# Decoder trunk step: the squares of k as two fp32r halves for their product with ones, and work reordered around it

## The chip, the cores and the metric

The kernel runs on one core of a Trainium2 chip. The metric is the device time of one execution in microseconds (us), median of the runs shown. TensorE multiplies matrices, VectorE (DVE), ScalarE (ACT) and GpSimd (POOL) do the elementwise work, SyncE (SP) issues the transfers. Each engine works through its own instructions in order, and semaphores order the engines against each other.

## The reference

One layer of a hybrid decoder for 512 prompt tokens and 8 x 8 sample tokens (576 columns), width 1024, 8 heads. What the change touches:

```python
qkv = jax.nn.silu(causal_dwconv(qkv_ext, conv_qkv_w))
k = l2norm(qkv[..., QK_WIDTH:2 * QK_WIDTH].reshape(B, L, N_HEADS, HEAD_K))
def l2norm(x):
    return x * lax.rsqrt(jnp.sum(x * x, axis=-1, keepdims=True) + EPS)
o, s_new = gated_delta_chunked(q, k, v, g, beta, s_delta)   # chunked delta rule per head
glu = glu_in[..., :CONF_WIDTH] * jax.nn.sigmoid(glu_in[..., CONF_WIDTH:])
c = causal_dwconv(conf_ext, conf_dw_w) + conf_dw_b          # 31 taps
```

Around it stand the input projection (1024 to 3072 + 16 + 5120 columns), a gated output norm per head, a LayerNorm with swish on the convolution branch, the output projection and a feed-forward block of 4096 with squared relu.

## The kernel before

Activations lie with channels on the 128 partitions and the 576 tokens along the row. Every dense product is made in a split form: both operands are cut into a high fp32r half and a low fp32r rest, and three products (high x high, low weights x high, high weights x low) are summed in PSUM. A job is one block of 128 output channels: 8 blocks of the inner dimension, 3 products, two halves of 288 columns, 48 products of TensorE. The weights' high half is a cast on ScalarE (`proj_split`, L1060), the low half a subtraction on GpSimd (L2026, 2.4 us).

**Passes.** After a first stage that projects head 1's inputs (`raw_job`), passes 1 to 8 follow. Pass n does the attention of head n while it projects the inputs of head n + 1, convolves them, and evacuates the gates of head n. Pass 1 and pass 8 are written out, passes 2 to 7 are one loop, on every engine. Each pass is a list of slots s = 0 to 31. In each slot TensorE first issues as many dense products as `MIDDLE_AT[s]` says (12, 12, 14, 14, ...), and then the small products of that slot (`phase`, from L705). The other engines walk through the same slots in the same order, each with its own conditions on s; the order is written out by hand.

**Around the product with ones** (the boundary of two passes):

- slot 29, TensorE: last state products (L846, L848). ScalarE copies the output o and squares it in PSUM (L1300, L1302).
- slot 30: DVE adds the q term to the squares (`o_sq`) and updates the sample states; then taps of the 31-tap convolution (`conf_taps`, L1605, counts per slot in `late` and `late_1`).
- slot 31: TensorE sums o's squares with a matrix of ones (`ones_sum`, L632, full fp32). ScalarE squares k (`square_k`, L1148), then takes the logarithm and the exponent that give o's factor; DVE scales o (`head_out`), then more taps.
- slot 0 of the next pass: TensorE sums k's squares with ones (L632, two full fp32 products of 288 columns). ScalarE, once `head_out` and the sums are there, makes k's factor (L1243, L1245). DVE copies the head's columns (L1799) and writes kn = kc * factor (L1655).
- slot 2: TensorE transposes kn (L722) and v (L700); in pass 1 v's transposes stand in slot 7. ScalarE copies v (L1248).

**Around slots 20 to 23.** In slot 20 GpSimd splits weights, then writes `gext`, the gated convolution input (L2167, L2168), and signals `gext_ready`. In slot 22 TensorE multiplies gk with u (L813) and the first chunk (L832); ScalarE negates and copies that into kn (L1270, `kd_ready`) and scales the chunk (`chunk_u`, L1184, `u_ready`). In slot 23 TensorE's first state product (L846) waits for both; the sample products (L858) follow.

**Entry of pass 1.** The last things of the first stage are DVE's read of v's projection and its 4-tap convolution (`read_qkv`, `qkv_conv`), and GpSimd's low halves of the input (`in_low`). TensorE's first job of pass 1 waits per block k for `in_ready`, and after 12 of its products for that read of v.

Of the kernel before, what the change touches and what calls it, by code (L numbers as in the profile page):

```python
# [25 lines left out]
F32 = mybir.dt.float32  # L26
# [5 lines left out]
P = 128  # L32
HP = P // 2
D = 1024
H = 8
# [45 lines left out]
_LAYOUT = [("zero", 1), ("ident", P), ("ident2", HP), ("ones", P), ("tri", P), ("suf", P), ("tri_s", SMP), ("suf_s", SMP),  # L81
# [14 lines left out]
def build(nc, x_t, w_all, w_log, log_par, consts, params, taps, halos, s_in,  # L96
          y_out, s_prompt, s_sample, qkv_rows, conf_rows):
    with ExitStack() as ctx:
# [3 lines left out]
        def sem(name):  # L102
# [9 lines left out]
                 ("gext", GXT + NS * GXS), ("c4", TOK), ("c31", TOK),  # L112
# [51 lines left out]
        csum = sb("csum", TOK)  # L164
        q_sq = sb("q_sq", TOK)
# [155 lines left out]
        k_sq, k_sums, k_scale, k_ready = sem("k_sq"), sem("k_sums"), sem("k_scale"), sem("k_ready")  # L321
# [245 lines left out]
        def _(pe):  # L567
# [22 lines left out]
            def dense(n, s):  # L590

                done = sum(spread(n)[:s])
                for i in range(done, done + spread(n)[s]):
                    j, r = divmod(i, PASS_MM)
                    h, r = divmod(r, PASS_MM // 2)
                    k, p3 = divmod(r, 3)
                    at, w = base(n) + j, w_buf(n, j)
                    if r == 0:
                        if h == 0:
                            pe.wait_ge(w_high, at + 1)  # L600
                            pe.wait_ge(w_low, at + 1)
                        if last(n) and j == 8:
                            pe.wait_ge(ln_scaled, KB)
                        elif last(n) and j == 9:
                            pe.wait_ge(act_read, 2 * at - 3 + h)
                        elif n_is(n, 1) and j == 0:
                            pe.wait_ge(pair_read, 4)
                        else:
# [17 lines left out]
            def ones_half(dst, src, start=True, stop=True):  # L626
                return mm(dst, con("ones"), src, start=start, stop=stop)

            def ones_sum(dst, src, start=True, stop=True):

                for h in range(2):
                    r = mm(dst[:, h], con("ones"), src[:, h * HALF:(h + 1) * HALF],  # L632
                           start=start, stop=stop)
                return r
# [70 lines left out]
            def phase(n):  # L705
                for s in range(32):
# [335 lines left out]
        def _(act):  # L1042
# [102 lines left out]
            def square_k(n):  # L1145

                act.wait_ge(act_conv, 3 * n + turn(n, 1) + 1)
                A(v["vt"][:, 0:TOK], v["kc"], ACT.Square).then_inc(k_sq, 1)  # L1148

# [42 lines left out]
            def phase(n):  # L1192
                for s in range(33):
# [52 lines left out]
                    if s == (7 if n_is(n, 1) else 2):  # L1246
                        act.wait_ge(kv_tr, 2 * n)
                        A(v["vt"][:, 0:SEQ], g(1), ACT.Copy)  # L1248
                        A(v["vts"][0:SMP], g(3)[0:SMP, 0:P], ACT.Copy).then_inc(vt_ready, 1)
# [4 lines left out]
                    if s in range(8, 19, 2):  # L1254
# [9 lines left out]
                        r.then_inc(x_ready, 1)  # L1264
                        if s == 8 and not last(n):
# [60 lines left out]
            square_k(0)  # L1326
# [145 lines left out]
        def _(dve):  # L1472
# [10 lines left out]
            ve.memset(v["gext"][:, 0:CF_TAPS - 1], 0.0)  # L1483
            ve.memset(csum[:], 0.0).then_inc(csum_done, 1)
# [130 lines left out]
            def qkv_conv(n, i, a, b):  # L1615
# [19 lines left out]
                if b == QK_TAPS:  # L1635
                    if i == 0 and not first(n):
                        dve.wait_ge(qd_ready, n)
                    dve.wait_ge(conv4_prod, 3 * n + at + 1)
                    ve.tensor_reduce(CONV[i][:, SEQ:TOK].rearrange("p (s a) -> p s a", s=NS), products(at),  # L1639
                                     mybir.AxisListType.X, ALU.add).then_inc(conv4, 1)  # L1640
                    dve.wait_ge(conv4, 15 * n + 5 * at + 5)
                    dve.sem_inc(conv4_done, 1)
# [114 lines left out]
            late_1 = {24: 4, 25: 2, 26: 3, 27: 2, 28: 2, 29: 1, 30: 4, 31: 4}  # L1757
            early_1 = {1: 3, 2: 1, 3: 3, 8: 2, 10: 1, 12: 1, 16: 1, 18: 1, 19: 2, 20: 2, 21: 2}

            def convolutions(n, s):  # L1760
                proj = not last(n)
                rest = early_8 if last(n) else early_1 if n_is(n, 1) else early
# [259 lines left out]
        def _(pool):  # L2022
# [83 lines left out]
            for k in range(4, KB):  # L2106
                in_low(k)
            pool.wait_ge(in_ready, KB)
# [5 lines left out]
            pool.wait_ge(act_read, 10)  # L2114
            qkv_rows_and_products(0, 2)
# [21 lines left out]
            def phase(n):  # L2137
# [6 lines left out]
                for s in range(33):  # L2144
# [73 lines left out]
                    if s == 19:  # L2218
# [3 lines left out]
                        tt(pr(v["um"]), pr(t_r.bitcast(F32)), bc(con("ident")), ALU.subtract).then_inc(tmi_ready, 1)  # L2222
                    if s == 26:
# [63 lines left out]
def shape_constants():  # L2287
# [15 lines left out]
    put("ones", np.ones((P, P)))  # L2303
# [100 lines left out]
```

## Time and profile before

| | us |
|---|---|
| median of 3 runs | 1101.4 |
| lowest and highest | 1097.24 and 1102.29 |
| the profiled execution | 1099.08 |
| its span in the trace | 1097.1 |

| engine | busy us | share of the span |
|---|---|---|
| PE (TensorE) | 1076.4 | 98% |
| DVE | 709.8 | 65% |
| ACT | 508.2 | 46% |
| POOL | 578.1 | 53% |

The profile is of one execution; its time is 2.3 us under the median. The mean granted clock of TensorE was 0.995 of full. A row of a timeline has the start in us, the length in us, the engine and line, the output and inputs by name, the shapes, a count, and in brackets the idle time ahead of it with what ended it. PE is TensorE's products, PEld its weight loads. A product of 288 columns is recorded about 0.3 us long, and the next one starts before it ends: the distance of starts is what it costs. A full fp32 product leaves two records.

### The profile page before, as it was taken

What the parts mean: (1) busy time and instruction counts of PE and PEld (TensorE: products, weight loads), DVE (VectorE), ACT (ScalarE), POOL (GpSimd) and SP (SyncE); (2) the same over time, 40 slices, a digit from 0 to 9 for tenths busy, and PEclk for the clock granted to TensorE, in tenths of its full rate; (3) what the DMA queues carried; (4) which work ended last, traced back from release to release, by engine and by line L of the source; (5) the groups of instructions that cost most, each with busy time, mean ns of one, the idle gap of its engine ahead of it and who ended that gap; (6) DMA issues with size and microseconds to landing.
All of it is one profiled execution on the core that took longest, in us unless ns stands there. A gap on an engine that the chain in (4) does not pass through costs nothing.

```text
span 1097.1 us, 22165 instructions
## 1 busy us (share of the span) xinstructions
PE 1076.4 (98%) x8279; PEld 1054.0 (96%) x8279; DVE 709.8 (65%) x1150; ACT 508.2 (46%) x918; POOL 578.1 (53%) x503
## 2 busy tenths in 40 slices
PE   8999999999999999999999999999999999999996
PEld 6899899999999999999999999999999999999996
DVE  7987987969879698797967757631243134216635
ACT  7844455554554555545746955321232123214531
POOL 1987385583855738557574432324333433436831
PEclk9999999999999999999999999999999999999998
DMA  6223112231122311223221252122232222223302
GB/s 239 95 65 108 62 40 90 80 106 61 38 90 78 106 61 42 86 78 106 81 73 44 64 218 77 59 78 77 78 94 80 78 83 89 76 76 96 98 21 86
DMA packets 32663, 92.12 MB, mean 84 GB/s; under 512 B 4704, under 2 KB 12256, under 8 KB 32608
## 3 DMA queue, kind: packets, MB, share of 16 engines
q1 hardware_dynamic: 32608, 91.36, 25.8%
q8 instruction: 38, 0.62, 0.2%
q14 instruction: 17, 0.14, 0.0%
HBM read 82.83 MB, written 8.52 MB: 83 GB/s over the span
## 4 chain that ended last, share of the span: by engine, by line
PE 87%; DVE 5%; issue 2%; ACT 1%; POOL 0%; DVEq 0%; ACTq 0%
PE ps L584 31%; PE ps L613 30%; PE ps L622 6%; PE ps L977 5%; DVE ps L1479 2%; DVE work L1476 1%; PE ps L805 1%; PE ps L858 1%; PE ps L795 1%; PE ps L774 1%; PE ps L867 1%; PE ps L832 1%; PE ps L813 1%; PE ps L846 1%; PE ps L848 1%
## 5 line engine op out<-in xcount | busy, mean ns | idle before, releaser
L2026 POOL TENSOR_TENSOR w_lo<-raw,w_hi 128x1024 fp32r<-128x1024 f32 x121 | 292.4, 2417 | 360.6 <-ACT w_hi L1078 231.0
L613 PE MATMUL ps<-in_hi,w_hi 128*128 128x288 f32 x944 | 287.6, 305 | 0.6 <-POOL in_lo L2026 0.6
L613 PE MATMUL ps<-in_hi,w_lo 128*128 128x288 f32 x944 | 284.4, 301 | 0.0
L613 PE MATMUL ps<-in_lo,w_hi 128*128 128x288 f32 x944 | 283.0, 300 | 0.0
L1479 DVE SCALAR_TENSOR_TENSOR ps<-work,ct,ps 128x512 f32<-128x512 f32 x240 | 180.7, 753 | 7.3 <-DVE work L1639 1.5
L613 PEld LDWEIGHTS ps<-in_hi,w_hi 128*128 128x128 f32 x944 | 178.0, 189 | 1.9 <-POOL in_lo L2026 0.9
L613 PEld LDWEIGHTS ps<-in_hi,w_lo 128*128 128x128 f32 x944 | 177.8, 188 | 0.9
L613 PEld LDWEIGHTS ps<-in_lo,w_hi 128*128 128x128 f32 x944 | 178.0, 189 | 0.2
L1078 ACT CAST w_hi<-raw 128x1024 fp32r<-128x1024 f32 x61 | 63.8, 1048 | 224.2 <-PE ps L584 224.2
L1476 DVE TENSOR_TENSOR f_tmp<-f_tmp 128x576 f32<-128x576 f32 x31 | 70.7, 2281 | 96.3 <-ACT f_tmp L1426 91.0
L1476 DVE TENSOR_TENSOR o_a<-o_a,ps 128x576 f32<-128x576 f32 (+1 forms) x40 | 25.3, 634 | 144.8 <-PE ps L584 122.8
L584 PE MATMUL ps<-in_hi,w_hi 128*128 128x288 f32 x464 | 99.4, 296 | 0.1
L584 PE MATMUL ps<-in_lo,w_hi 128*128 128x288 f32 x464 | 99.4, 296 | 0.0
L584 PE MATMUL ps<-in_hi,w_lo 128*128 128x288 f32 x464 | 99.3, 296 | 0.0
L584 PE MATMUL ps<-f_lo,w_hi 128*128 128x288 f32 x384 | 82.5, 296 | 0.0
L584 PE MATMUL ps<-f_hi,w_hi 128*128 128x288 f32 x384 | 82.5, 296 | 0.0
L584 PE MATMUL ps<-f_hi,w_lo 128*128 128x288 f32 x384 | 82.5, 296 | 0.0
L584 PEld LDWEIGHTS ps<-in_hi,w_hi 128*128 128x128 f32 x464 | 74.7, 189 | 0.3 <-issue 0.3
L584 PEld LDWEIGHTS ps<-in_hi,w_lo 128*128 128x128 f32 x464 | 74.8, 189 | 0.0
L584 PEld LDWEIGHTS ps<-in_lo,w_hi 128*128 128x128 f32 x464 | 74.7, 189 | 0.0
L1060 ACT CAST w_hi<-raw 128x1024 fp32r<-128x1024 f32 x63 | 65.6, 1042 | 0.0
L584 PEld LDWEIGHTS ps<-f_hi,w_hi 128*128 128x128 f32 x384 | 61.8, 189 | 0.0
(312 smaller groups left out, 2291.9 us busy)
## 6 DMA issues: line engine op xcount, KB each, us to landing
raw<-w_all_in SPq DMA_DIRECT2D x135, 512.0 KB, 3.6
work<-s_in_in SPq DMA_DIRECT2D x8, 512.0 KB, 3.2
s_sample_out<-work SPq DMA_DIRECT2D x8, 512.0 KB, 2.7
xt<-x_t_in SPq DMA_DIRECT2D x4, 576.0 KB, 6.7
xt<-x_t_in SPq DMA_DIRECT2D x2, 1152.0 KB, 7.1
y_out<-o_a SPq DMA_DIRECT2D x16, 144.0 KB, 1.7
halo<-halos_in SPq DMA_DIRECT2D x9, 156.0 KB, 3.5
conf_rows_out<-c_rows SPq DMA_DIRECT2D x8, 135.0 KB, 2.1
```

The source lines that it names most:

```text
L584: r = mm(ps[:, 2 * w + h, 0:HALF], a[:, k], b[:, k, h * HALF:(h + 1) * HALF], start=k == 0 and p3 == 0, stop=k == KB - 1 and p3 == 2)
L613: t = mm(dense_ps(n, j, h), a[:, w, k], b[:, k, h * HALF:(h + 1) * HALF], start=r == 0, stop=r == PASS_MM // 2 - 1)
L622: r = mm(dst, a[:, k], half_of(b[:, k], h), start=k == 0 and p3 == 0, stop=k == KB - 1 and p3 == 2)
L774: r = mm(tile(g(0), c)[0:HP], cut(w, c), tile(t_r, c), start=True, stop=True)
L795: r = mm(tile(g(0), c)[0:HP], cut(uc_r, c), tile(x_r, c), start=True, stop=True)
L805: r = mm(cut(g(1), c), tile(x_r, c), cut(uc_r, c), start=True, stop=True)
L977: r = mm(half_ps(i % 4), a[:, k], half_of(b[:, k], h), start=k == 0 and p3 == 0, stop=k == KB - 1 and p3 == 2)
L1060: nc.scalar.copy(w_hi[:, w_buf(n, j)], raw[:, raw_slot(n, j)]).then_inc(w_high, 1)
L1078: nc.scalar.copy(weight(m, off)[0], raw[:, (off + 2) % RING]).then_inc(w_high, 1)
L1476: return ve.tensor_tensor(out, a, b, op)
L1479: return ve.scalar_tensor_tensor(out=out, in0=a, scalar=s_, in1=b, op0=op0, op1=op1)
L2026: return gp.tensor_tensor(out, a, b, op)
```

## The change

From pass 2 on the squares of k are formed in slot 21 (24 in pass 1) of the pass before: ScalarE writes them twice, as fp32r (`ksq_hi`, on the place of c4) and as fp32 (on the place of extk), GpSimd subtracts in slot 22 (25) to get the low half (`ksq_lo`, on the place of c31), and TensorE sums four fp32r products. The square in slot 31 is gone. The places require waits: the squares for `gext_ready`, the subtraction for `conf_ready`, the halo copies for the product with ones.

With it come: the matrix of ones is set by DVE instead of loaded; in the first half of pass 1's first job the 16 products with the high input come first and wait for `high_ready`, the 8 with the low input last; v's transposes in pass 1 stand in slot 8, and its copies behind those of the first level; v's sample sum (`qkv_samples`) and one tap stand behind kn in slot 0 of pass 1, and one tap more behind v's convolution; pass 1 has 18 of its own taps in place of 22, and pass 2, now written out on DVE, takes the other four in slots 8, 10, 12 and 16; GpSimd forms v's sample products ahead of its memsets.

```diff
@@ dense (TensorE)
+                    low_last = n_is(n, 1) and j == 0 and h == 0
+                    if low_last:
+                        k, p3 = divmod(r, 2) if r < 2 * KB else (r - 2 * KB, 2)
...
-                    if n_is(n, 1) and j == 0 and h == 0 and p3 == 0:
+                    if low_last and p3 == 0:
+                        pe.wait_ge(high_ready, k + 1)
+                    if low_last and p3 == 2:
                         pe.wait_ge(in_ready, k + 1)
@@ TensorE
+            def ones_pair(dst, hi, lo):
+                for h in range(2):
+                    mm(dst[:, h], ones_r[:], half_of(hi, h), start=True, stop=False)
+                    r = mm(dst[:, h], ones_r[:], half_of(lo, h), start=False, stop=True)
                 return r
...
-                        ones_sum(g2(0), v["vt"]).then_inc(k_sums, 1)
+                        if n_is(n, 1):
+                            ones_sum(g2(0), v["vt"]).then_inc(k_sums, 1)
+                        else:
+                            ones_pair(g2(0), ksq_hi, ksq_lo).then_inc(k_sums, 1)
...
-                    if n_is(n, 1) and s == 7:
+                    if n_is(n, 1) and s == 8:
                         pe.wait_ge(act_conv, 3)
                         pe.wait_ge(qk_ready, 1)
                         v_transposes()
@@ ScalarE
+            def square_k_pair(n):
+                act.wait_ge(act_conv, 3 * n + 3)
+                act.wait_ge(gext_ready, n + 1)
+                A(ksq_hi[:], v["kc"], ACT.Square)
+                A(ksq, v["kc"], ACT.Square).then_inc(k_high, 1)
...
+            def v_tile(n):
+                act.wait_ge(kv_tr, 2 * n)
+                A(v["vt"][:, 0:SEQ], g(1), ACT.Copy)
+                A(v["vts"][0:SMP], g(3)[0:SMP, 0:P], ACT.Copy).then_inc(vt_ready, 1)
...
+                        if s == 8 and n_is(n, 1):
+                            v_tile(n)
                         if s == 8 and not last(n):
                             conv_silu(n, 0)
+                    if s == (24 if n_is(n, 1) else 21) and not last(n):
+                        square_k_pair(n)
                     if s == 22:
...
                     if s == 31 and not last(n):
                         log_exp()
-                        square_k(n)
@@ DVE
+            ve.memset(ones_r[:].bitcast(F32), 1.0)
...
-            late_1 = {24: 4, 25: 2, 26: 3, 27: 2, 28: 2, 29: 1, 30: 4, 31: 4}
-            early_1 = {1: 3, 2: 1, 3: 3, 8: 2, 10: 1, 12: 1, 16: 1, 18: 1, 19: 2, 20: 2, 21: 2}
+            late_1 = {24: 4, 25: 2, 26: 3, 27: 2, 28: 2, 29: 1, 30: 2, 31: 2}
+            early_1 = {1: 3, 2: 1, 3: 3, 8: 2, 10: 1, 12: 1, 16: 1, 18: 1, 19: 2, 20: 2, 21: 1}
+            early_2 = {1: 3, 2: 1, 3: 3, 8: 3, 10: 1, 12: 1, 16: 1}
...
+                    if n_is(n, 1) and s == 0:
+                        dve.wait_ge(in_ready, KB)
                     head(n, s)
+                    if n_is(n, 1) and s == 0:
+                        conf_taps(0, 12, 13)
+                        qkv_samples(0, 2)
...
-            conf_taps(0, 10, 12)
+            conf_taps(0, 10, 11)
             read_qkv(2)
             qkv_conv(0, 2, 0, QK_TAPS)
+            conf_taps(0, 11, 12)
             phase(1)
-            with dve.Fori(2, H) as n:
+            phase(2)
+            with dve.Fori(3, H) as n:
@@ GpSimd
+            pool.wait_ge(act_read, 10)
+            qkv_rows_and_products(0, 2)
             pool.wait_ge(in_ready, KB)
...
                         pool.wait_ge(conv4_done, 3 * n)
+                        pool.wait_ge(k_sums, n)
                         pool.nop(nofuse=True)
                         halo_copies(n)
...
+                    if s == (25 if n_is(n, 1) else 22) and proj:
+                        pool.wait_ge(k_high, n)
+                        pool.wait_ge(conf_ready, n)
+                        tt(ksq_lo[:], ksq, ksq_hi[:].bitcast(F32), ALU.subtract).then_inc(k_sq, 1)
```

## Rows read from the trace of the kernel before

**Rows 1.** the chain of work that ended last: L858 in three passes (start us, us, what)
```profile
106.54 1.69 PE ps L858 x16
...
178.45 1.69 PE ps L858 x16
...
246.47 1.69 PE ps L858 x16
```

**Rows 2.** timeline of TensorE in slot 0 of pass 3 (start us, us, engine, line)
```profile
195.52 1.14 PE L632 MATMUL ps<-work,cst 128*128 128x288 f32 x4
...
196.63 0.29 PE L613 MATMUL ps<-in_hi,w_lo 128*128 128x288 f32 x1
...
196.76 0.29 PE L613 MATMUL ps<-in_lo,w_hi 128*128 128x288 f32 x1
```

**Rows 3.** timeline, end of pass 2 to slot 2 of pass 3, and the wait one pass later
```profile
191.98 0.82 DVE L1476 TENSOR_TENSOR work<-ps,q_sq 128x512 f32<-128x512 f32 x2 [0.44 <-ACT ps L1302]
...
200.23 0.66 PE L722 MATMUL ps<-cst,work 128*128 128x128 f32 x4
...
201.92 0.30 PE L613 MATMUL ps<-in_hi,w_hi 128*128 128x288 f32 x1
...
268.23 0.42 PEld L722 LDWEIGHTS ps<-cst,work 128*128 128x128 f32 x4 [0.35 <-DVE work L1476]
```

**Rows 4.** timeline of DVE and TensorE between pass 1 and pass 2
```profile
122.28 3.12 DVE L1479 SCALAR_TENSOR_TENSOR ps<-work,ct,ps 128x512 f32<-128x512 f32 x4
...
126.83 3.12 DVE L1479 SCALAR_TENSOR_TENSOR ps<-work,ct,ps 128x512 f32<-128x512 f32 x4
...
127.98 0.29 PE L613 MATMUL ps<-in_hi,w_lo 128*128 128x288 f32 x1
...
130.76 1.12 PE L722 MATMUL ps<-cst,work 128*128 128x128 f32 x4 [2.49 <-DVE work L1476]
...
133.89 0.29 PE L613 MATMUL ps<-in_hi,w_hi 128*128 128x288 f32 x1
```

**Rows 5.** engines' busy time by stretch; last three: granted clock, DMA share, GB/s
```profile
49.00:58.40 9.40, 6.91 (x45) 5.92 (x43) 6.60 (x13) 6.46 (x9) 9.34 (x13) 1.00 0.29 94
...
130.70:133.90 3.20, 3.13 (x15) 3.06 (x16) 3.10 (x6) 0.70 (x2) 2.39 (x7) 0.51 0.05 18
```

**Rows 6.** timeline of TensorE and GpSimd at the entry of pass 1
```profile
51.60 1.21 PE L632 MATMUL ps<-work,cst 128*128 128x288 f32 x4 [0.62 <-DVE work L1476]
...
54.62 0.40 PE L613 MATMUL ps<-in_hi,w_hi 128*128 128x288 f32 x1 [0.63 <-POOL in_lo L2026]
...
56.90 2.36 POOL L2026 TENSOR_TENSOR w_lo<-raw,w_hi 128x1024 fp32r<-128x1024 f32 x1
...
58.37 0.66 PE L722 MATMUL ps<-cst,work 128*128 128x128 f32 x4 [1.22 <-DVE work L1476]
...
60.30 0.29 PE L613 MATMUL ps<-in_hi,w_hi 128*128 128x288 f32 x1
...
72.06 0.63 PE L700 MATMUL ps<-cst,work 128*128 128x128 f32 x4 [0.87 <-DVE work L1476]
```

**Rows 7.** timeline of slots 20 to 23 of pass 2, all engines
```profile
174.83 1.55 POOL L2026 TENSOR_TENSOR work<-work 128x512 f32<-128x512 f32 x2
...
176.16 0.60 ACT L1270 ACTIVATE work<-ps 128x512 f32<-128x512 f32 x1 [4.72 <-PE ps L814]
...
176.41 0.75 DVE L1602 TENSOR_SCALAR ps<-work,ct 128x512 f32<-128x512 f32 x1 [1.84 <-POOL work L2026]
...
176.76 0.37 ACT L1184 ACTIVATE work<-ps,hc 128x128 f32<-128x128 f32 x1
...
177.71 0.32 PEld L846 LDWEIGHTS ps<-work 128*128 128x128 f32 x2
```

**Rows 8.** timeline of ScalarE, slot 31 of pass 2
```profile
193.58 0.69 ACT L1148 ACTIVATE work<-work 128x576 f32<-128x576 f32 x1
...
194.17 0.72 ACT L1307 ACTIVATE work<-ps,cst 128x576 f32<-128x576 f32 x1
```

More of the change, by code:

```diff
@@ L78 @@
 STORE_ORDER = (range(8), (3, 4, 0, 5, 1, 6, 7, 2))
-_LAYOUT = [("zero", 1), ("ident", P), ("ident2", HP), ("ones", P), ("tri", P), ("suf", P), ("tri_s", SMP), ("suf_s", SMP),
+_LAYOUT = [("zero", 1), ("ident", P), ("ident2", HP), ("tri", P), ("suf", P), ("tri_s", SMP), ("suf_s", SMP),
            ("eps", 1), ("epsq", 1), ("big", P), ("big_s", SMP), ("lvl", (LEVELS - 1) * HP),
@@ L111, in build @@
                  ("extq", EXT + NS * EXS), ("extk", EXT + NS * EXS), ("extv", EXT + NS * EXS),
-                 ("gext", GXT + NS * GXS), ("c4", TOK), ("c31", TOK),
+                 ("gext", GXT + NS * GXS + 1), ("c4", TOK), ("c31", TOK),
                  ("qc", TOK), ("kc", TOK), ("vc", TOK),
@@ L164, in build @@
         csum = sb("csum", TOK)
+        ones_r = sb("ones_r", P, F32R)
+        ksq_hi = nc.alloc_sbuf_tensor_at("ksq_hi", [P, TOK], F32R, offset=work_at + 4 * (5 * SEQ + starts["c4"]))
+        ksq_lo = nc.alloc_sbuf_tensor_at("ksq_lo", [P, TOK], F32R, offset=work_at + 4 * (5 * SEQ + starts["c31"]))
+        ksq = v["extk"][:, 4:4 + TOK]
         q_sq = sb("q_sq", TOK)
@@ L320, in build @@
         hc_ready, gm_ready, w_part_landed = sem("hc_ready"), sem("gm_ready"), sem("w_part_landed")
-        k_sq, k_sums, k_scale, k_ready = sem("k_sq"), sem("k_sums"), sem("k_scale"), sem("k_ready")
+        k_high, k_sq, k_sums, k_scale, k_ready = sem("k_high"), sem("k_sq"), sem("k_sums"), sem("k_scale"), sem("k_ready")
         conv4_prod = sem("conv4_prod")
@@ L595, in dense @@
                     h, r = divmod(r, PASS_MM // 2)
-                    k, p3 = divmod(r, 3)
+                    low_last = n_is(n, 1) and j == 0 and h == 0
+                    if low_last:
+                        k, p3 = divmod(r, 2) if r < 2 * KB else (r - 2 * KB, 2)
+                    else:
+                        k, p3 = divmod(r, 3)
                     at, w = base(n) + j, w_buf(n, j)
@@ L626, in ones_half @@
             def ones_half(dst, src, start=True, stop=True):
-                return mm(dst, con("ones"), src, start=start, stop=stop)
+                return mm(dst, ones_r[:].bitcast(F32), src, start=start, stop=stop)
             def ones_sum(dst, src, start=True, stop=True):
                 for h in range(2):
-                    r = mm(dst[:, h], con("ones"), src[:, h * HALF:(h + 1) * HALF],
+                    r = mm(dst[:, h], ones_r[:].bitcast(F32), src[:, h * HALF:(h + 1) * HALF],
                            start=start, stop=stop)
+                return r
+            def ones_pair(dst, hi, lo):
+                for h in range(2):
+                    mm(dst[:, h], ones_r[:], half_of(hi, h), start=True, stop=False)
+                    r = mm(dst[:, h], ones_r[:], half_of(lo, h), start=False, stop=True)
                 return r
@@ L716, in phase @@
                         pe.wait_ge(k_sq, n)
-                        ones_sum(g2(0), v["vt"]).then_inc(k_sums, 1)
+                        if n_is(n, 1):
+                            ones_sum(g2(0), v["vt"]).then_inc(k_sums, 1)
+                        else:
+                            ones_pair(g2(0), ksq_hi, ksq_lo).then_inc(k_sums, 1)
                     if s == 2:
@@ L1143, in conv_silu, with square_k @@
                 A(CONV[i][:, SEQ:TOK], CONV[i][:, SEQ:TOK], ACT.Silu).then_inc(act_conv, 1)
-            def square_k(n):
-                act.wait_ge(act_conv, 3 * n + turn(n, 1) + 1)
+            def square_k():
+                act.wait_ge(act_conv, 1)
                 A(v["vt"][:, 0:TOK], v["kc"], ACT.Square).then_inc(k_sq, 1)
+            def square_k_pair(n):
[3 more added lines that the diff above has]
+                A(ksq, v["kc"], ACT.Square).then_inc(k_high, 1)
             def square_q(n):
@@ L1245, in phase @@
                         A(g2(0), two(v["at"]), ACT.Exp, scale=-0.5).then_inc(k_scale, 1)
[L1246 to L1249, printed above, removed]
+                    if s == 2 and not n_is(n, 1):
+                        v_tile(n)
                     if s == 3:
@@ L1264, in phase @@
                         r.then_inc(x_ready, 1)
+                        if s == 8 and n_is(n, 1):
+                            v_tile(n)
                         if s == 8 and not last(n):
                             conv_silu(n, 0)
+                    if s == (24 if n_is(n, 1) else 21) and not last(n):
+                        square_k_pair(n)
                     if s == 22:
@@ L1325, in _ @@
             conv_silu(0, 1)
-            square_k(0)
+            square_k()
             read_by_dve(4)
@@ L1634, in qkv_conv, with qkv_samples @@
                     stt(out, e[:, t:t + SEQ], w, out, ALU.mult, ALU.add).then_inc(conv4, 1)
[L1635 to L1642, printed above, removed]
+                if b == QK_TAPS and not (first(n) and i == 2):
+                    qkv_samples(n, i)
+            def qkv_samples(n, i):
+                at = turn(n, i)
+                if i == 0 and not first(n):
+                    dve.wait_ge(qd_ready, n)
+                dve.wait_ge(conv4_prod, 3 * n + at + 1)
+                ve.tensor_reduce(CONV[i][:, SEQ:TOK].rearrange("p (s a) -> p s a", s=NS), products(at),
+                                 mybir.AxisListType.X, ALU.add).then_inc(conv4, 1)
+                dve.wait_ge(conv4, 15 * n + 5 * at + 5)
+                dve.sem_inc(conv4_done, 1)
             def sample_state(n):
@@ L1756, in _ @@
             late = {22: 2, 23: 2, 24: 4, 25: 2, 26: 2, 27: 2, 28: 2, 29: 1, 30: 3, 31: 2}
-            late_1 = {24: 4, 25: 2, 26: 3, 27: 2, 28: 2, 29: 1, 30: 4, 31: 4}
-            early_1 = {1: 3, 2: 1, 3: 3, 8: 2, 10: 1, 12: 1, 16: 1, 18: 1, 19: 2, 20: 2, 21: 2}
+            late_1 = {24: 4, 25: 2, 26: 3, 27: 2, 28: 2, 29: 1, 30: 2, 31: 2}
+            early_1 = {1: 3, 2: 1, 3: 3, 8: 2, 10: 1, 12: 1, 16: 1, 18: 1, 19: 2, 20: 2, 21: 1}
+            early_2 = {1: 3, 2: 1, 3: 3, 8: 3, 10: 1, 12: 1, 16: 1}
             def convolutions(n, s):
                 proj = not last(n)
-                rest = early_8 if last(n) else early_1 if n_is(n, 1) else early
+                rest = early_8 if last(n) else early_1 if n_is(n, 1) else early_2 if n_is(n, 2) else early
                 if s in rest:
@@ L2113, in _ @@
             gate_rows()
-            pool.wait_ge(act_read, 10)
-            qkv_rows_and_products(0, 2)
             proj_split(1, 1)
@@ L2302, in shape_constants @@
     put("ident2", i[:, :HP] % HP == j[:, :HP])
-    put("ones", np.ones((P, P)))
     put("tri", i <= j)
```

## The prediction

> **What bounds the kernel now.** I read the chain that ended last first: the sixteen small products of the sample state (L858) stand in it once per pass, 71.91 us apart from pass 1 to 2 and 68.02 us from 2 to 3 [rows 1]. Later passes repeat the 68.0 us, so the first step is 3.9 us longer. TensorE is busy nearly all of the span, so the question is what TensorE waits for, and second, whether work taken off it lies where it would wait anyway.
>
> The steady boundary of two passes, as TensorE sees it: product of k's squares with ones in slot 0, 26 dense products, then the transposes of the scaled k (L722), which wait 0.35 us on the DVE product that writes kn [rows 3]. That product is the end of a row of DVE work without a hole: from 191.98 (the first add of the output's squares, which waits for ScalarE's square of o, itself released by the last state product of slot 29) to about 200.2, where TensorE starts [rows 3]. Nothing in it waits for the product with ones.
>
> The same place between pass 1 and 2 is worse: four taps at 122.28 and four at 126.83 stand in DVE's row, TensorE stops for 2.49 us, and its next rows take 3.13 us (130.76 to 133.89) where pass 3 takes 1.69 us (200.23 to 201.92) [rows 3, 4]. The window over that stretch shows the granted clock at 0.51, the lower level of 1.2 GHz [rows 5]. At the entry of pass 1 there are three waits (0.62, 0.63, 1.22 us) and one of 0.87 us at the transposes of v [rows 6], all at a granted clock of 1.00 [rows 5].
>
> **The change, part by part.**
>
> *The product itself.* In the old form, from 195.52 to 196.63 lie the four records of two full fp32 products and one dense product; dense products follow each other at 0.13 us (196.63 to 196.76; over longer stretches 0.133). So the two cost 1.11 - 0.13 = 0.98 us [rows 2]. Four fp32r products of the same shape are four dense steps, 0.53 us. That frees 0.45 us of TensorE in each of seven passes. In passes 3 to 8 this is worth nothing: TensorE comes to the transposes of k 0.45 us earlier and waits 0.35 + 0.45 = 0.80 us for the same kn [rows 3]. If that cover were absent it would be 6 x 0.45 = 2.7 us. I take 0, and keep 2.7 for the range. (The Trainium skill, FP8 and Floating Point Precision, section TensorE Precision Notes, says a true fp32 product is four passes through the array. By that the two would be eight passes of 288 columns against four: an estimate of 0.48 us saved at 2.4 GHz, against 0.45 from the rows. The page alone, without asking who waits next, would give 7 x 0.48 = 3.4 us off the time. That is a rival below.)
>
> *The squares move on ScalarE.* In slot 31 one square goes; ScalarE's result is not waited for there (DVE's row has no hole there), so 0. In slot 21 (24 in pass 1) two squares come in, behind a wait for the gated values gext. This I take to be the costly step. In the steady pass gext ends at 174.83 + 1.55 = 176.38, and DVE, which waits for the same semaphore, starts at 176.41 [rows 7]. ScalarE's next work now starts at 176.16: kn's negated copy, and 0.60 us behind it the first chunk of u, done at 177.13 [rows 7]. TensorE wants both at 177.71, for the first state product [rows 7]. With the pair in front, the squares start at 176.42, each 0.59 us behind the other (193.58 to 194.17 for such a square [rows 8]), so the copy starts at 177.60, u is there at 178.57, and TensorE goes on at about 178.63: a wait of 0.92 us. Behind it on ScalarE come a table load and the reads of z, which have over a microsecond of room. All later steps of the pass hang on TensorE, DVE's taps too, and the end chain is counted from slot 29, so nothing gives the 0.92 back. Six passes (2 to 7): +5.5 us. Bounds: 0 if the pair finds gext earlier, and +6.4 if a square with fp32r output has a pitch of 0.67. In pass 1 the pair stands in slot 24, in a hole of 1.39 us ahead of the second chunk: 0.
>
> *The low half on GpSimd*: one subtraction of 1.4 us in slot 22 (25 in pass 1), where GpSimd is idle for some 4.8 us ahead of its next weight split; it hides there. Its result is wanted 15 us later. The halo copies' wait for the product with ones is over by the time they are due.
>
> *DVE's taps.* Pass 1 loses four taps of 0.78 us in slots 30 and 31, and pass 2 takes them in slots 8, 10, 12 and 16, where DVE waits 0.4 to 1.1 us for TensorE; pass 1 already carries such taps there without stopping it. The tap moved from slot 21 has room too. At the boundary: o is scaled at 123.84 instead of 125.31, head_out at 125.4, two taps to 126.95, kn from 127.05 to 127.75. TensorE gets there at 127.98 + 0.13 - 0.45 = 127.7. So the transposes start near 127.8 instead of 130.76: 2.97 us. With no long stop the clock stays up: 3.13 - 1.69 = 1.44 us more [rows 3, 4]. Together -4.4 us; bounds -2.5 and -4.4.
>
> *Entry of pass 1.* One tap less ahead of v's read: the wait of 0.62 goes. High products first in the first half: at 54.62 only one product of three is left, 0.27 us. kn no longer stands behind v's sample sum, which waited for GpSimd: it runs from 54.65 to 55.4, and TensorE arrives at 56.74 instead of 58.37, 1.63 us ahead. But the low weights of the second job still end at 56.90 + 2.36 = 59.26 on GpSimd, and that job's first product (60.30 before) would now be due at 58.67: a new wait of 0.7, and 0.94 us are left [rows 6]. The wait of 0.87 at v's transposes goes (slot 8). The copies of v now stand behind the first level's copies on ScalarE and hold TensorE in slot 9 for about 0.5. Sum -1.2 us; bounds -0.3 (the low weights and v's copies later than I think) and -2.5.
>
> *Ones from a memset, a longer DVE program, a smaller constants transfer*: at the start, where other loads end last: 0.
>
> Sum: -1.2 - 4.4 + 5.5 = -0.1 us on the profiled 1099.1 us (span 1097.1), which lies 2.3 us below the median of 1101.4. I forecast 1101.3. The bounds together: -0.3 - 2.5 + 6.4 = +3.6, so 1105; and -2.5 - 4.4 - 2.7 + 0 = -9.6, so 1091.8.
>
> **Rivals.** About 0.5% (5.5 us) is what a measurement can tell here; the three runs of before are 5 us apart.
>
> A. *The pair costs nothing on ScalarE.* For: ScalarE has 4.7 us idle ahead of the copy. Against: that hole ends before gext does [rows 7]. Then only the gains: 1101.4 - 5.6 = 1095.8, right at the bound. Chance 0.17.
>
> B. *The product's gain counts in each pass as well* (the page's sum, 3.4 us, or mine of 0.45 x 7 less the one already counted). It needs a shorter DVE row at the boundary. Against: that row is not touched in the loop. With A, 1101.4 - 5.6 - 2.7 = 1093; without A, 1098.6, no change by the bound. Chance 0.05 with A, 0.04 alone.
>
> C. *The clock falls once a pass.* TensorE would wait 0.9 us in slot 23, and near 0.25 and 0.8 at the boundary. If those drop the clock as the 2.49 us stop did, each pass pays 1.44 us more: 6 x 1.44 = 8.6, so 1110, slower. It decides from four such passes on. Against: 1.22 us alone, with two of 0.6 before it inside 7 us, left the clock at 1.00 [rows 5, 6]. Chance 0.07. (The Trainium skill, TensorE: Matmul & The Clock Gate, section A second HAM failure mode, says that frequent small idles between groups of products can make the clock go back and forth. No row here shows that; rows show only the fall after 2.49 us.)
>
> D. *The rebalancing fails*: the four taps in pass 2 stop TensorE there, or the stop at the boundary stays, and ScalarE's wait comes on top. +5.5 - 1.2 and perhaps +1: 1106, about the bound. Chance 0.09.
>
> The forecast has 0.58. Faster: half of A and B with A, and a little, 0.15. Slower: C and a third of D, 0.11. The same: 0.74. The range runs from A to D, 1095.5 to 1106.0, some 0.83.
>
> **What the changed profile would show.** The small products of slot 23 about 68.9 us apart in passes 2 to 7 (68.0 if A), with a wait of TensorE of 0.9 us at the first state product in slot 23, released by ScalarE, and an idle time on ScalarE ahead of the squares that ends on GpSimd; the wait at the transposes of k near 0.8 us; pass 2 no longer at clock 0.51; a wait on GpSimd's weights near 59 us and on ScalarE's copy of v near 75 us. Wrong would be: no wait in slot 23, or a clock under 1.00 in the loop.

## The result and the profile after

The changed kernel takes 1105.7 us (median of 20 runs, 1101.3 to 1110.3), the kernel before, in runs between them on the same chip, 1101.5 us (20 runs, 1097.2 to 1102.4). The ratio is 1.0040 with a 95% interval of 1.0027 to 1.0053: slower by 4 us, beyond the interval, though under the 0.5% that the text called measurable. The forecast was 1101.3, the same. The profiled execution took 1101.7 us (span 1099.9) at a granted clock of 0.993; that of before had 1099.1, 1097.1 and 0.995. So the two profiled executions lie 2.6 us apart, the medians 4.2. The account by trace below is of these two executions; both are among the short ones of their kernel, and no profile here is of an execution near either median.

The chain that ended last, of the changed kernel (start us, us, what). The small products of slot 23 are L878 here, L858 in [rows 1]; they are eight fp32 products of 16 columns, which leave sixteen records:

```profile
105.42 1.69 PE ps L878 x16
...
174.28 1.69 PE ps L878 x16
...
243.18 1.69 PE ps L878 x16
...
313.68 1.69 PE ps L878 x16
...
382.58 1.69 PE ps L878 x16
...
451.50 1.69 PE ps L878 x16
...
522.01 1.69 PE ps L878 x16
...
602.47 1.69 PE ps L878 x16
```

The first line is 1.12 us earlier than in [rows 1]. The step from pass 1 to 2 is 68.86 and no longer 71.91: the slow boundary is gone. The next steps are 68.90 where 68.0 stood, and two of them, from 243.18 and from 451.50, are 70.50.

What the weight loads of TensorE waited for, all passes (us in total, times, longest), the lines of slot 23 and of k's transposes:

```profile
PEld ps L866 <- ACT work L1211: 5.2, 6, 0.9
PEld ps L742 <- DVE work L1509: 4.1, 5, 0.8
```

Six waits of 0.87 us on ScalarE, at the first state product. The timeline of pass 3 around slot 23, against [rows 7] one pass earlier:

```profile
238.66 1.55 POOL L2073 TENSOR_TENSOR work<-work 128x512 f32<-128x512 f32 x2
...
240.24 0.76 DVE L1636 TENSOR_SCALAR ps<-work,ct 128x512 f32<-128x512 f32 x1 [1.83 <-POOL work L2073]
240.30 0.69 ACT L1174 ACTIVATE ksq_hi<-work 128x576 fp32r<-128x576 f32 x1 [5.03 <-POOL work L2073]
...
240.89 0.67 ACT L1175 ACTIVATE work<-work 128x576 f32<-128x576 f32 x1
...
241.47 0.58 ACT L1304 ACTIVATE work<-ps 128x512 f32<-128x512 f32 x1
...
242.05 0.37 ACT L1211 ACTIVATE work<-ps,hc 128x128 f32<-128x128 f32 x1
...
242.47 0.49 PE L866 MATMUL ps<-work 128*128 128x128 f32 x2 [0.63 <-ACT work L1211]
...
243.02 1.86 PE L878 MATMUL ps<-work 128*128 128x16 f32 x16
...
245.34 0.30 PE L623 MATMUL ps<-in_hi,w_lo 128*128 128x288 f32 x1
...
245.47 0.40 PE L623 MATMUL ps<-in_lo,w_hi 128*128 128x288 f32 x1
...
245.68 0.44 PE L623 MATMUL ps<-in_hi,w_hi 128*128 128x288 f32 x1
...
245.91 0.44 PE L623 MATMUL ps<-in_hi,w_lo 128*128 128x288 f32 x1
```

This is the queue that was forecast: both squares start when GpSimd's gated values are there, 0.59 us behind each other, the negated copy (L1304) and the chunk of u (L1211) behind them, and TensorE behind that. The last four lines are what was not forecast: dense products step by 0.13 us up to 245.47 (from 245.34), and then by 0.21 and 0.23.

The windows of that stretch and of pass 6, and of the old slow boundary (columns as in [rows 5]):

```profile
246.00:248.00 2.00, 2.00 (x11) 2.00 (x11) 1.93 (x3) 0.46 (x2) 0.00 (x0) 0.50 0.00 0
...
454.00:456.00 2.00, 2.00 (x11) 2.00 (x10) 1.93 (x3) 0.33 (x1) 0.00 (x0) 0.50 0.00 0
128.00:131.00 3.00, 3.00 (x26) 3.00 (x25) 2.97 (x7) 0.69 (x2) 0.89 (x5) 1.00 0.24 91
```

The clock falls to its lower level of 1.2 GHz (0.50 of full) for a while from 245.5 and again some 210 us later, in two passes of six, and each fall costs 70.50 - 68.90 = 1.60 us. The boundary of [rows 5], at 0.51 before, runs at 1.00.

The account by trace, to the last L878: -1.1 (first line), -3.9 (the 71.91 that became a normal 68.0), +5.3 (six waits), +3.2 (two falls), -0.1 in the last step: +3.4, measured 602.47 - 599.06 = 3.4. Behind it the changed kernel is 0.6 shorter, so the span is 2.8 longer.

### The profile page after: what moved, and what is told of

Read it like the earlier page. It is cut to its first block, busy times and chain, and to the rows that moved or that the text cites. A ratio compares the mean times of both kernels' runs of the same rounds, so it can differ in the third digit from the quotient of the medians.

```text
span 1099.9 us, 22125 instructions
## 1 busy us (share of the span) xinstructions
PE 1076.0 (98%) x8279; PEld 1053.8 (96%) x8279; DVE 709.3 (64%) x1151; ACT 512.2 (47%) x925; POOL 588.9 (54%) x510
## 4 chain that ended last, share of the span: by engine, by line
PE 79%; POOL 6%; issue 5%; DVE 4%; ACT 3%; DVEq 0%; ACTq 0%; POOLq 0%
PE ps L588 31%; PE ps L623 25%; PE ps L632 6%; PE ps L997 5%; POOL w_lo L2073 2%; DVE ps L1512 2%; POOL work L2073 2%; PE ps L878 1%; POOL o_a L2073 1%; PE ps L825 1%; DVE work L1509 1%; POOL in_lo L2073 1%; PE ps L866 1%; PE ps L887 1%; PE ps L815 1%
## 5 line engine op out<-in xcount | busy, mean ns | idle before, releaser
L588 PEld LDWEIGHTS ps<-f_hi,w_lo 128*128 128x128 f32 x384 | 61.8, 189 | 0.0
```

The source lines that it names most:

```text
L588: r = mm(ps[:, 2 * w + h, 0:HALF], a[:, k], b[:, k, h * HALF:(h + 1) * HALF], start=k == 0 and p3 == 0, stop=k == KB - 1 and p3 == 2)
```

## The experiments

"Behind" and "ahead" are places in ScalarE's order. Runs of the kernel before between them gave medians of 1101.9, 1101.8 and 1101.3.

**1. The squares behind the chunk of u.** From pass two on the pair is issued in slot 22 behind the first chunk.

```diff
-                    if s == (24 if n_is(n, 1) else 21) and not last(n):
+                    if n_is(n, 1) and s == 24:
                         square_k_pair(n)
...
                         chunk_u(n, (s - 22) // 2)
+                    if s == 22 and not n_is(n, 1) and not last(n):
+                        square_k_pair(n)
```

> The changed kernel with the two squares of passes 2 to 7 moved from ahead of slot 22's copies on ScalarE to behind the scaling of the first chunk of u. Theory: the wait of TensorE at the first state product of slot 23 (six of about 0.9 us) goes, and with it the falls of the clock behind it; steps of L878 go from 68.9 and 70.5 us back to 68.0; time 1101.4 - 5.6 = about 1095.8, ratio to before 0.995. Rival 1 (the waits cost only their own length, and the clock falls for another reason): falls stay, about 1100. Rival 2 (the product's 0.45 us counts in each pass): another 2.7 us less, about 1093.

Median 1098.8 (12 runs, 1093.2 to 1099.5), ratio 0.9969 (0.9952 to 0.9987), span of the profiled run 1091.7 at clock 0.997. The chain of it:

```profile
105.20 1.69 PE ps L878 x16
...
173.19 1.69 PE ps L878 x16
...
241.20 1.69 PE ps L878 x16
```

Steps of 68.0, no wait at L866, and in this execution no fall of the clock in any pass. The order on ScalarE is the cause of the waits, and the falls go with them. But the runs come in two groups, 1093.2 to 1093.7 (4) and 1098.5 to 1099.5 (8), which no theory so far had. The 1095.8 expected lies in the empty stretch between them.

**2. The fp32 product back, all else as changed.** No pair, no subtraction; the single square in slot 31 as before.

```diff
-                        if n_is(n, 1):
-                            ones_sum(g2(0), v["vt"]).then_inc(k_sums, 1)
-                        else:
-                            ones_pair(g2(0), ksq_hi, ksq_lo).then_inc(k_sums, 1)
+                        ones_sum(g2(0), v["vt"]).then_inc(k_sums, 1)
...
+                        A(v["vt"][:, 0:TOK], v["kc"], ACT.Square).then_inc(k_sq, 1)
```

> The changed kernel without its title: one square in slot 31 and two full fp32 products with ones in each pass, as before; everything else of the change stays. Theory: the rest of the change is worth 5.6 us and the product itself nothing, so the same time as the kernel with the squares behind the chunk, about 1095.8; the wait at the transposes of k in passes 3 to 8 is 0.35 us instead of 0.8. Rival (the product counts in each pass): 2.7 us more than that kernel.

1099.2 (12 runs, 1094.0 to 1099.8), ratio 0.9972 (0.9954 to 0.9990). Level with run 1, and again two groups: 1094.0 to 1094.1 (3) and 1098.2 to 1099.8 (9). Its profiled execution fell into the upper group, and so shows what makes it. The timeline of DVE and GpSimd before pass 1:

```profile
46.14 2.43 POOL L2070 TENSOR_TENSOR w_lo<-raw,w_hi 128x1024 fp32r<-128x1024 f32 x1
...
47.62 6.46 DVE L1836 COPY hc<-cols 128x30 f32<-128x30 f32 x1
...
48.51 5.52 POOL L2070 TENSOR_TENSOR in_lo<-xt,in_hi 128x576 fp32r<-128x576 f32 x4
...
54.00 0.74 DVE L1509 SCALAR_TENSOR_TENSOR ps<-work,ct,ps 128x512 f32<-128x512 f32 x1
```

and the same copy in the profiled execution of the changed kernel, which is of the lower group:

```profile
48.32 0.97 DVE L1839 COPY hc<-cols 128x30 f32<-128x30 f32 x1
...
49.22 5.55 POOL L2073 TENSOR_TENSOR in_lo<-xt,in_hi 128x576 fp32r<-128x576 f32 x4
```

A copy of 30 columns takes 6.46 us instead of 0.97 and ends with GpSimd's row of four subtractions. The sum with ones that k's scale hangs on waits behind it, 5.3 us by the list of waits, and the clock is at its lower level when TensorE goes on (window):

```profile
56.00:58.00 2.00, 2.00 (x5) 1.43 (x6) 1.89 (x4) 0.92 (x1) 2.00 (x6) 0.50 0.00 0
```

The shorter copy, too, ends only with the GpSimd instruction that was running when it came, the weight split before the row; in later passes the same copy takes 0.18 us.

**3. The pair alone, on the kernel before.** Squares in slot 21, subtraction, four fp32r products with a matrix of ones set by DVE, and GpSimd's wait; the taps and the entry of pass 1 stay as before.

```diff
+                    if s == (24 if n_is(n, 1) else 21) and not last(n):
+                        square_k_pair(n)
...
-                        square_k(n)
```

> The kernel before with the title of the change alone: the two squares in slot 21 (24 in pass 1), the subtraction on GpSimd and four fp32r products; taps, entry of pass 1 and v's transposes as before. Theory: six waits of 0.9 us (+5.5 us), a fall of the clock behind some of them (+1.6 us each, 2 to 5 of 6), and nothing gained: 1101.4 + 5.5 + 3 to 8 = 1110 to 1115. If the falls need the rest of the change: 1107. If the product counts: 2.7 less.

1109.0 (6 runs, 1105.6 to 1111.0), ratio 1.0075 (1.0049 to 1.0100), 1 us under the 1110 to 1115 expected. The waits of it, matmuls:

```profile
PE ps L736 <- DVE work L1498: 7.2, 7, 2.9
PE ps L860 <- ACT work L1205: 3.8, 6, 0.6
```

The six waits are there, the stop of the first boundary (2.9) too, and the clock falls in two passes again (behind 247 and 386). But behind the long stop itself it does not fall (timeline and window):

```profile
130.54 0.66 PE L736 MATMUL ps<-cst,work 128*128 128x128 f32 x4 [2.94 <-DVE work L1498]
```

```profile
130.00:132.00 2.00, 1.46 (x13) 1.46 (x14) 1.93 (x4) 0.11 (x1) 2.00 (x3) 1.00 0.09 35
```

The kernel before, with a stop of 2.49 at this place, was at 0.51 there [rows 5]. The pair by itself costs 1109.0 - 1101.9 = 7 us; the rest of the change earns some 3 to 5 of it back (7.0 less the 4.2 of the result, and 1.1 + 3.9 by the account).

**4. One square ahead, one behind.** The changed kernel, with only the fp32r square left in slot 21 from pass two on.

```diff
                 A(ksq_hi[:], v["kc"], ACT.Square)
+                if n_is(n, 1):
+                    square_k_full()
+
+            def square_k_full():
                 A(ksq, v["kc"], ACT.Square).then_inc(k_high, 1)
...
                         chunk_u(n, (s - 22) // 2)
+                    if s == 22 and not n_is(n, 1) and not last(n):
+                        square_k_full()
```

> The changed kernel with only the fp32r square ahead of slot 22's copies in passes 2 to 7, the full one behind the first chunk. Theory: the wait in slot 23 is 0.9 - 0.6 = 0.3 us, six times (+1.9 us over the kernel with both behind), about 1097.7 if a wait so short leaves the clock alone. Rival (the clock falls at any added wait in slot 23): falls in some passes as in the changed kernel, 1100 to 1105.

1101.1 (12 runs; groups 1095.2 and 1100.5 to 1101.9), ratio 0.9989 (0.9972 to 1.0006), 2.3 us above run 1. In the profiled execution the six waits are 1.8 us together, the steps 68.3, and the clock stays up. Six waits of 0.3 us cost 6 x 0.3 and little more, those of 0.9 cost 6 x 0.9 and the falls.

**5 to 7. The copy of head 1's columns on ScalarE**, in the kernel before (5), the changed kernel (6), and run 1's kernel (7).

```diff
-            dve.wait_ge(log_dve, 6)
-            head_cols(1)
...
             square_q(0)
+            act.wait_ge(log_dve, 6)
+            act.wait_ge(next_ready, 1)
+            act.wait_ge(cols_ready, 2)
+            A(hc[:].unsqueeze(2), cols[:].rearrange("p (a h) -> p a h", h=H)[:, :, 0:1],
+              ACT.Copy).then_inc(hc_ready, 1)
```

> The kernel before with one edit: head 1's column copy (128 x 30, DVE) at the end of the first stage is made by ScalarE instead. In the profile of the kernel without the pair that copy lasted 6.46 us, until GpSimd's row of subtractions had a hole, where it took 0.97 us in the profiles of before and of the changed kernel; the times of before lie in two groups, near 1097.4 and near 1101.9. Theory: the copy makes the two groups (a copy on DVE is held by GpSimd's work and slips in between two subtractions or doesn't); on ScalarE only one group is left, 1096 to 1098, median 4 us under before. Rival: the groups have another cause; they stay and the median too.

> The changed kernel with the same edit (head 1's columns copied by ScalarE). Theory: without the copy's two groups the spread that is left is that of the clock's falls behind slot 23, each about 1.6 us: 1093.5 + 5.5 = 1099 with none, 1100.6, 1102.2, 1103.8, 1105.4, up to 1108.6 with six. Median near 1102 (two falls). Rival: the falls come from the copy's late state; then all runs lie at 1099.

> Squares behind the chunk and head 1's columns on ScalarE. Theory: neither the waits of slot 23 nor the copy's late state: one group at 1092 to 1094, ratio to before 0.992. Rival: the two groups stay (1093.5 and 1099).

Run 5: 1098.36 (5 runs, 1098.15 to 1098.48), ratio 0.9964 (0.9951 to 0.9978). Run 6: 1101.6 (11 runs, 1099.9 to 1103.3), ratio 1.0000 (0.9988 to 1.0013). Run 7: 1093.8 (5 runs, 1093.1 to 1093.9), ratio 0.9922 (0.9909 to 0.9936). The copy in run 5, on its new engine:

```profile
49.49 0.25 ACT L1335 ACTIVATE hc<-cols 128x30 f32<-128x30 f32 x1
```

One group each in 5 and 7, 0.3 and 0.8 us wide, where there were two some 4 to 6 us apart (in runs 9 to 11, which have the same edit, again one each). So DVE's copy is what splits the runs. With it out of the way the three kernels stand 1098.4, 1101.6, 1093.8: the change costs 3.2 us, and with the squares behind the chunk it would have earned 4.5. Run 6 alone stays wide. Its profile shows the clock down behind 174 and behind 382, other passes than in the changed kernel's (window, of the second):

```profile
384.00:386.00 2.00, 2.00 (x11) 2.00 (x11) 1.90 (x3) 0.00 (x0) 0.00 (x0) 0.51 0.00 0
```

Its runs' mean clocks go from 0.996 in the shortest to 0.990 in the longest, which fits a varying number of falls.

Slot 23 of pass 3 in run 7 (timeline), where the chunk (L1211) is first and the squares lie behind it, under TensorE's work:

```profile
239.73 0.37 ACT L1211 ACTIVATE work<-ps,hc 128x128 f32<-128x128 f32 x1
...
239.98 0.69 ACT L1174 ACTIVATE ksq_hi<-work 128x576 fp32r<-128x576 f32 x1
...
240.81 0.38 PE L866 MATMUL ps<-work 128*128 128x128 f32 x2
```

**8. A wait among dense products.** Run 7's kernel, and in passes 2 to 7 a wait in the middle of slot 7's dense products for a value of DVE's.

```diff
+                    if s == 7 and i == done + 12 and not isinstance(n, int):
+                        pe.wait_ge(qk_ready, n)
```

> The kernel of the run before this one (squares behind the chunk, columns on ScalarE) with a wait of TensorE put into passes 2 to 7 inside the dense products of slot 7: it waits there for DVE's qk, some 0.9 us, with dense products on both sides, where the changed kernel waits 0.9 us with small fp32 products right behind. Theory (the fall needs the small products of slot 23 behind the wait): 6 x 0.9 = 5.5 us more, 1099 in every run, granted clock 1.00 in the loop. Rival (any such wait can make the clock fall): a spread of several steps of 1.6 us as in the changed kernel, median near 1102.

1101.2 (11 runs, 1100.4 to 1101.6), ratio 0.9991 (0.9982 to 1.0000). The timeline at one such wait, and the windows around it:

```profile
208.33 0.29 PE L625 MATMUL ps<-in_hi,w_lo 128*128 128x288 f32 x1
209.68 0.19 PEld L625 LDWEIGHTS ps<-in_lo,w_hi 128*128 128x128 f32 x1 [1.29 <-DVE work L1518]
209.68 0.40 PE L625 MATMUL ps<-in_lo,w_hi 128*128 128x288 f32 x1 [1.06 <-DVE work L1518]
```

```profile
209.00:212.00 3.00, 2.32 (x18) 2.32 (x19) 2.73 (x6) 0.01 (x1) 2.84 (x7) 1.00 0.11 44
212.00:215.00 3.00, 3.00 (x30) 3.00 (x29) 1.64 (x4) 2.39 (x5) 3.00 (x5) 1.00 0.00 0
```

The waits are longer than those of slot 23 (1.1 to 1.3 us against 0.9), six as well, and cost 1101.2 - 1093.8 = 7.3 us, 1.2 each, where 0.9 each was expected: their own length and no more. No run's mean clock is under 0.996, and no window in the loop is under 1.00. So the length of a wait alone does not decide whether the clock falls.

**9. The fp32 product with run 2's and run 5's edits together.**

> The rest of the change without its title (one square in slot 31, full fp32 products), head 1's columns on ScalarE. Theory (the product's 0.45 us lies under the wait for kn): the same as the kernel with the squares behind the chunk and the same copy, 1093.8, one group; it comes 0.45 us earlier in pass 2 alone at most. Rival (the product counts in each pass): 1096.5.

1093.7 (6 runs, 1093.3 to 1093.8), ratio 0.9941 (0.9925 to 0.9956). Run 7, the same but for the pair, has 1093.8: four fp32r products for two fp32 ones are worth nothing here. In the list of waits the transposes of k wait 4.0 us in five passes in run 7, and 1.8 in run 9: what the product saves is waited for, as forecast.

**10 and 11. One tap off the row that sets the boundary**, moved from slot 30 to slot 8, with the pair (10) and without it (11).

```diff
-            early = {1: 3, 2: 1, 3: 3, 8: 2}
-            early_8 = {1: 3, 2: 2, 6: 2, 8: 2}
-            late = {22: 2, ..., 29: 1, 30: 3, 31: 2}
+            early = {1: 3, 2: 1, 3: 3, 8: 3}
+            early_8 = {1: 3, 2: 2, 6: 2, 8: 3}
+            late = {22: 2, ..., 29: 1, 30: 2, 31: 2}
```

> The squares behind the chunk, columns on ScalarE, and one tap of passes 2 to 7 moved from slot 30 to slot 8 of the next pass, so that o is scaled and k's factor made earlier. Theory: the DVE row ahead of kn is 0.78 us shorter, TensorE's wait of 0.8 us at the transposes of k goes nearly, six times: 1093.8 - 4.5 = 1089.3; here the pair product's gain shows. Rival (k's factor waits for something else): no change, 1093.8.

> The same moved tap with full fp32 products and the square in slot 31. Theory: the wait at k's transposes is only 0.35 us here, so 6 x 0.35 = 2.1 us are gained: 1091.7; the difference to the kernel with the pair, 0.45 us a pass (2.7 us), is the product's own gain. Rival (the product gains nothing even then): both the same.

Run 10: 1090.8 (5 runs, 1090.5 to 1091.3), ratio 0.9917 (0.9899 to 0.9935). Run 11: 1091.9 (6 runs, 1091.6 to 1092.4), ratio 0.9926 (0.9911 to 0.9942). The transposes of k, list of waits of run 10:

```profile
PEld ps L742 <- DVE work L1516: 1.0, 4, 0.2
```

The wait shrinks from 4.0 us in all to 1.0, and the time by 3.0. A tap is 0.78 us, so 4.5 were expected: the wait of a pass went from 0.81 to 0.25 (0.56, not 0.78), so the row is still the longer side, and 0.2 of the tap is lost elsewhere in it, which was not followed up. Run 11 has no such wait left and gains 1.75 of the 1.8 that run 9 waited. The product is now worth 1.1 us, not the 2.7 of six full savings.

**12. Run 7 with the taps of before** in passes 1 and 2.

```diff
-            late_1 = {24: 4, ..., 29: 1, 30: 2, 31: 2}
+            late_1 = {24: 4, ..., 29: 1, 30: 4, 31: 4}
...
-                rest = ... early_2 if n_is(n, 2) else early
+                rest = ... early
```

> The squares behind the chunk, columns on ScalarE, but four taps back in slots 30 and 31 of pass 1 (four and four) and none of them in pass 2. Theory: the stop of 2.5 us at k's transposes of pass 2 is back (a little longer, by the 0.45 us of the product) and the clock at 1.2 GHz behind it; 1093.8 + 4.4 = 1098.2. If the clock stays up: 1096.8. Rival (the taps cost nothing): 1093.8.

1097.2 (12 runs, 1095.6 to 1098.5), ratio 0.9971 (0.9959 to 0.9984), 3.3 us above run 7. The stop is back, in the timeline:

```profile
128.90 0.81 PE L742 MATMUL ps<-cst,work 128*128 128x128 f32 x4 [2.94 <-DVE work L1516]
```

And here the clock falls behind it, where it did not behind the same 2.94 in run 3 (window):

```profile
130.00:132.00 2.00, 2.00 (x11) 1.92 (x10) 1.97 (x4) 0.75 (x2) 1.23 (x5) 0.50 0.00 0
```

The step from pass 1 to 2 is 72.02 against 67.99 in run 7, so the taps are worth 4.0 there; 0.8 of it is not seen in the time, since the first L878 came at 104.67 against 105.43. That first line lies anywhere from 104.7 to 105.4 in the nine kernels that share its pass 1 so far and have no held copy, so 0.7 us of each comparison by single traces is chance. The three shortest runs of this kernel (1095.6 to 1096.2) have a mean clock of 0.997, seven of the nine others 0.994 or 0.995: in these three, too, the clock may have stayed up.

## Why the prediction came out as it did

*The product itself, 0: right.* The four products take 0.52 us in a row in the profile after, from the first ones product to the next dense one (timeline of pass 4):

```profile
261.81 0.29 PE L649 MATMUL ps<-ksq_hi,ones_r 128*128 128x288 f32 x1
...
262.20 0.29 PE L650 MATMUL ps<-ksq_lo,ones_r 128*128 128x288 f32 x1
...
266.51 0.42 PEld L742 LDWEIGHTS ps<-cst,work 128*128 128x128 f32 x4 [0.81 <-DVE work L1509]
```

The last line is the one of [rows 3] that had 0.35: forecast 0.80. Runs 7 and 9 show that nothing reaches the time, and runs 10 and 11 what it needs: a shorter DVE row. Rival B is out.

*Two squares ahead of the chunk, +5.5: right.* Six waits, 5.2 us in the list, 5.3 by the steps, and run 1 takes them away by order alone. Rival A is out. (The "sixteen small products" of the text are eight, with two records each; nothing in the sum hangs on it.)

*The taps, -4.4: right in kind, 0.5 too much.* The stop is gone, TensorE starts the transposes at 126.6 without a wait, the windows stand at 1.00, and the step is 3.9 us shorter before the new wait is counted. The 1.44 us of it that are the clock's are there to gain only where the clock had fallen: behind a stop as long it fell in run 12 and not in run 3. Of the ten runs of the kernel before that stood between the others and took under 1098 us, nine had a mean clock of 0.997, against 0.995 in its profile, so it probably does not fall in every execution of that kernel either. D's stop in pass 2 is not there.

*Entry of pass 1, -1.2: right in size, to the tenth by luck.* -1.1 by the chain; the parts named in the text add up to -1.3, and single traces of the same entry differ by 0.7. The two new waits are there, on the second job and at v's first tiles (timeline, pass 1; 0.7 and 0.5 were forecast):

```profile
54.82 0.19 PEld L623 LDWEIGHTS ps<-in_lo,w_hi 128*128 128x128 f32 x1 [1.18 <-POOL in_lo L2073]
...
59.42 0.19 PEld L623 LDWEIGHTS ps<-in_hi,w_hi 128*128 128x128 f32 x1 [0.70 <-issue]
...
74.90 0.32 PEld L815 LDWEIGHTS ps<-x_r,uc_r 128*64 128x64 f32 x4 [0.75 <-issue]
```

The first line is a wait that was not counted: the low inputs, not the weights, end last there.

*The step that failed is the dismissal of rival C.* The text said that "1.22 us alone, with two of 0.6 before it inside 7 us, left the clock at 1.00", and gave falls a chance of 0.07. The clock does fall behind slot 23's wait, in two passes of six in each of three profiled executions (the changed kernel, runs 3 and 6); a clock under 1.00 in the loop was the sign of being wrong that the text named. The runs of run 6 reach from 1099.9 to 1103.3; run 7 plus six waits would be 1093.8 + 5.4 = 1099.2, so they hold between none and two or three falls. C priced a fall at 1.44 from the first boundary; it measured 1.60. So C came true for about a third of its passes in the profiled execution (+3.2), and the time ended between the forecast and C.

The row it was set aside by is a wait ahead of four transposes, with dense products behind them [rows 6]. Run 8 puts a wait of 1.1 to 1.3 us among dense products in each pass, and the clock stays. Slot 23 is a wait of 0.9, then two fp32 products of 128 columns, then the eight of 16 (1.86 us). Runs 1 and 7 have the same small products without the wait, and run 4 has them with a wait of 0.3: there is no fall in their traces. So among waits of about a microsecond every fall came behind one that small products followed; small fp32 products of 128 columns also lie shortly ahead of the wait (238.7 to 240.1 in pass 3), and no run tells the two apart. What picks the passes is not settled, nor why the same stop of 2.94 lowers the clock in run 12 and not in run 3. No run put a wait of 0.9 behind the small products, or filled them with dense ones. (The Trainium skill, TensorE: Matmul & The Clock Gate, section A second HAM failure mode, tells of a clock that goes back and forth where TensorE idles shortly between groups of products. Here it does, in some passes, though the page speaks of frequent idles and here two short waits stand in a pass of 69 us; the prediction set that sentence aside because no row of before showed it.)

*The base, +2.3.* The sum was made on a profiled execution of 1099.1 and carried to the median of 1101.4 by adding the difference, without knowing what it was. It is in the main the copy: both profiled executions, of before and after, have it in 0.97 us, while 17 of 20 runs of before and 13 of 20 of the changed kernel lie in their upper groups. A held copy costs 4.5 us up to the first small products of slot 23 (109.52 in run 2, 104.98 in run 9), more than the 2.3, and the rest of that difference is not explained. Adding it was right in size, but it is not the same for both kernels: the upper groups' medians are 1101.6 and 1107.0, 5.4 apart, the lower ones' 1098.1 and 1102.3, 4.2 apart. By run 1's upper group, 1099.0, and six waits, 5.3, the upper group of the changed kernel holds some 1.7 falls in the median (an estimate, from (1107.0 - 1099.0 - 5.3) / 1.6; no profile here is of that group). With the copy moved the difference is 3.2 us (runs 5 and 6).

## What to carry to other kernels

Before taking work off the busiest engine, ask what it waits for next: here 0.45 us per pass went into a wait for another engine's row, while the work that the saving needed stood ahead of a copy that TensorE was waiting for. Put helper work on a side engine behind whatever the critical engine needs next, even if there is a long hole in front of it: the hole ends with the input of the helper work. A wait that left the clock alone in one place, or in one execution, says nothing about another; look at what runs around it, and if single runs of a kernel fall into groups, find the instruction that differs before adding the difference to a forecast.

## What was not expected of the hardware

A DVE copy of 128x30 can be held for 5.5 us, through four instructions of GpSimd with two inputs each. It starts while GpSimd's weight split of 2.43 us still runs; in the profiled executions of the lower group it gets through before the next row (0.97 us), in the one of the upper group (run 2) only when that row is over (6.46 us), and so the same program runs some 4 to 6 us longer. With no GpSimd work beside it, it takes 0.18 us. ScalarE does the copy in 0.25 us beside the same row, and the groups are gone. (The Trainium skill, SBUF — State Buffer, section Who interferes with whom, says that DVE in a mode that uses both ports and GpSimd take a shared pair of ports for a whole instruction, and that the second to come is blocked fully. The traces agree in kind, though none shows which mode the copy ran in; in run 2's trace the blocked copy waits out the instructions behind the one that blocked it as well.)

The clock of TensorE fell behind waits of 0.9 us in some passes and not in others of one execution, and in none behind waits of 1.1 to 1.3 us among dense products. Even a stop of 2.94 us ahead of the same transposes lowered it in one execution (0.50, run 12) and not in another (1.00, run 3). In the loop the price of a fall was 1.6 us each time.

Best of the kernels run is that of run 10: 1090.8 us, 1% under the kernel before. It keeps the pair, has the squares behind the chunk, head 1's column copy on ScalarE, and one tap in slot 8 instead of 30.
